# Second mixer of a two-block transformer kernel: the second value tile projected last and turned inside the attention

## What is computed

```
q, k, v, qi, ki, wi = split(h @ w_in)      # 16 query heads, 4 key heads, 4 value heads of 64; 8 index heads
q, k = rope(rmsnorm(q)), rope(rmsnorm(k));  qi = rope(qi);  ki = rope(layernorm(ki))
score[t, s] = sum_h relu(qi[t, h] . ki[s]) * wi[t, h]      # causal
sel = top_k(score[t], 128)                                  # keys kept for token t
p = softmax(q . k / 8 over the selected keys);  o = p @ v;  out = o @ w_out
```

## Time and profile before

| what | value |
|---|---|
| median of 3 runs | 2035.12 us (2034.83 to 2035.23) |
| the profiled execution's own time | 2035.02 us |
| its span in the profile | 2033.2 us |
| TensorE busy | 2019.3 us, 99% of the span |
| VectorE busy | 1569.3 us, 77% |
| ScalarE busy | 1012.6 us, 50% |
| GpSimd busy | 264.9 us, 13% |
| chain that ended last | 89% TensorE, 7% VectorE, 2% ScalarE |
| projection of the second mixer ends, its attention ends | at about 1023 and 1113 us |

### The profile page before, as it was taken

The page is one execution under the profiler, slowest core; times in us unless marked ns, Lnnn a source line. Parts: engine busy times, 40 slices in busy tenths (PEclk is TensorE's granted clock), DMA queues, the critical chain, the costliest instruction groups (busy, mean ns, idle before and its releaser), DMA issues.

```text
span 2033.2 us, 35256 instructions
## 1 busy us (share of the span) xinstructions
PE 2019.3 (99%) x12600; PEld 1763.5 (87%) x12600; DVE 1569.3 (77%) x2377; ACT 1012.6 (50%) x1798; POOL 264.9 (13%) x254
## 2 busy tenths in 40 slices
PE   9999999999999999999999999999999999999999
PEld 8999988886889998877766889998888888999987
DVE  8789876897688988775987688888777668888822
ACT  6455632568455556234577455555233234555621
POOL 0021022650200301124311200001200000000000
PEclk9999999999999999999999999999999999999999
DMA  4233476330323335734310323335836522333332
GB/s 170 91 111 104 144 257 239 122 98 2 93 78 108 109 99 176 258 115 120 100 36 1 94 83 104 103 98 179 287 129 193 171 92 78 99 103 103 106 97 87
DMA packets 76474, 245.81 MB, mean 121 GB/s; under 512 B 9408, under 2 KB 9664, under 8 KB 76256
## 3 DMA queue, kind: packets, MB, share of 16 engines
q1 hardware_dynamic: 61376, 189.60, 30.1%
q0 software_dynamic: 15008, 55.06, 8.2%
HBM read 237.74 MB, written 2.62 MB: 118 GB/s over the span
## 4 chain that ended last, share of the span: by engine, by line
PE 89%; DVE 7%; ACT 2%; issue 1%; DMA 0%; ACTq 0%; SPq 0%; DVEq 0%
PE ps L879 17%; PE ps L881 16%; PE ps L880 16%; PE ps L979 12%; PE ps L978 12%; PE ps L977 12%; DVE ps L2527 1%; PE ps L1205 1%; DVE tmp L2029 1%; DVE small L2421 1%; PE ps L1226 1%; PE ps L1243 1%; PE ps L1368 0%; DVE ssum L1997 0%; DVE score L2634 0%
## 5 line engine op out<-in xcount | busy, mean ns | idle before, releaser
L1452 ACT ACTIVATE w_hi<-w_raw 128x1024 fp32r<-128x1024 f32 (+2 forms) x231 | 211.4, 917 | 245.5 <-PE ps L881 244.9
L879 PE MATMUL ps<-h_hi,w_hi 128*128 128x512 f32 x768 | 304.4, 396 | 0.0
L881 PE MATMUL ps<-h_hi,w_lo 128*128 128x512 f32 x768 | 299.4, 390 | 0.0
L880 PE MATMUL ps<-h_lo,w_hi 128*128 128x512 f32 x768 | 299.2, 390 | 0.0
L1987 DVE TENSOR_TENSOR w_lo<-w_raw,w_hi 128x768 fp32r<-128x768 f32 (+2 forms) x196 | 196.4, 1002 | 89.5 <-ACT w_hi L1452 83.7
L979 PE MATMUL ps<-h_hi,w_lo 128*128 128x256 f32 x840 | 237.7, 283 | 0.0
L978 PE MATMUL ps<-h_lo,w_hi 128*128 128x256 f32 x840 | 237.7, 283 | 0.0
L977 PE MATMUL ps<-h_hi,w_hi 128*128 128x256 f32 x840 | 237.7, 283 | 0.0
L978 PE MATMUL ps<-t_lo,w_hi 128*128 128x256 f32 x832 | 235.5, 283 | 0.0
L977 PE MATMUL ps<-t_hi,w_hi 128*128 128x256 f32 x832 | 235.5, 283 | 0.0
L979 PE MATMUL ps<-t_hi,w_lo 128*128 128x256 f32 x832 | 235.5, 283 | 0.0
(11 more groups left out here) (393 smaller groups left out, 4538.2 us busy)
## 6 DMA issues: line engine op xcount, KB each, us to landing
w_raw<-in_gate SPq DMA_DIRECT2D x88, 512.0 KB, 3.5
w_raw<-in_up SPq DMA_DIRECT2D x88, 512.0 KB, 4.4
h_over<-in_ada_w POOLq DMA_DIRECT2D x53, 512.0 KB, 5.3
w_raw<-in_down SPq DMA_DIRECT2D x64, 384.0 KB, 3.7
ada_raw<-in_ada_w POOLq DMA_DIRECT2D x43, 512.0 KB, 4.9
w_raw<-in_down SPq DMA_DIRECT2D x64, 320.0 KB, 4.2
w_raw<-in_w_mix_c SPq DMA_DIRECT2D x24, 512.0 KB, 3.9
w_raw<-in_w_mix_b SPq DMA_DIRECT2D x17, 512.0 KB, 3.6
```

The costliest lines, as they stand in the source:

```text
L879: pe.matmul(dest, s_hi, m_hi, start=first and n == 0, stop=False)
L880: pe.matmul(dest, s_hi, m_lo, start=False, stop=False)
L881: mm = pe.matmul(dest, s_lo, m_hi, start=False, stop=last and n == len(pairs) - 1)
L1452: act.activation(w_hi[:, cut], w_raw[:, cut], ACT.Copy).then_inc(w_hi_done, 1)
```

## The change

Three things change, and nothing of what is computed.

1. vB1 becomes the last tile, so the list is ki, wi, qi0 to qi3, vB0, kB0, kB1, qB0 to qB7, vB1. The key and query tiles are projected one place earlier. vB1's product goes to bank 7, its copy to a part of `relu`, and it is turned in step 1 of the attention; the head sum of qB7 falls into vB1's job, and the roots and the table load come before ScalarE waits for that job. The unread products go to bank 6, since bank 7 holds vB1.
2. The rope of a key tile comes 5 places after the tile (before 4), so it stays in steps 12 and 13; those of the query tiles move one step earlier, to steps 11 to 17. The rope of qB7 is taken apart: one of its three operations in each of the steps 1, 2 and 3 of the attention.
3. In `TOPS_AT` steps 10 and 11 have one round less each, and steps 17 and 18, which had none, have one each. The total ahead of the attention stays at 30.

The diff, cut to its core:

```diff
-        TILES_B = ["ki", "wi", "qi0", "qi1", "qi2", "qi3", "vB0", "vB1", "kB0", "kB1"] + [f"qB{t}" for t in range(8)]
+        TILES_B = ["ki", "wi", "qi0", "qi1", "qi2", "qi3", "vB0", "kB0", "kB1"] + [f"qB{t}" for t in range(8)] + ["vB1"]
...
-            return at + 4 if t[0] == "k" else at + 2
+            if t == "qB7":
+                return at + 3
+            return at + {"kA": 4, "kB": 5}.get(t[:2], 2)
...
-                return bank(TILES_B.index(t) % 4)
+                return bank(7 if t == "vB1" else TILES_B.index(t) % 4)
...
-        TOPS_AT = {8: (0, 1), 9: (4, 1), 10: (5, 2), 11: (4, 1), 12: (0, 2), 13: (3, 0), 14: (3, 0), 15: (2, 0), 16: (2, 0)}
+        TOPS_AT = {8: (0, 1), 9: (4, 1), 10: (5, 1), 11: (3, 1), 12: (0, 2), 13: (3, 0), 14: (3, 0), 15: (2, 0), 16: (2, 0),
+                   17: (1, 0), 18: (1, 0)}
...
             for m in range(2, len(TILES_B)):
                 tile_job(TILES_B, "mixB", m, 3, betweenB)
-            betweenB(len(TILES_B), 0)
-
...
+                if pair == PAIRS_B[2]:
+                    after(pe, v_done, "vB1")
...
             def sumsB(u):
+                if u == 1:
+                    turn_tile(TILES_B, len(TILES_B) - 1)
...
-            attention(PAIRS_B, scoreB, lambda pair: pair_turn(pair, pB, T, matsB), valuesB, sumsB, "stdB", 5)
+            attention(PAIRS_B, scoreB, lambda pair: pair_turn(pair, pB, T, matsB), valuesB, sumsB, "stdB", 5, 6)
...
                 t = TILES_B[m - 1]
+                if t == "vB1":
+                    query_std("B", 8 * len(QUERIES[1]))
+                    exp_table()
+                    after(act, i_sum, IDX[-1])
                 act.wait_ge(job_done, J + m + RING)
...
-            query_std("B", 8 * len(QUERIES[1]))
-            exp_table()
-            attention(PAIRS_B, pB, T, pTB, qscB, lambda u: None)
+            def keep_last(u):
+
+                if u == 1:
+                    keep_tile("vB1", len(TILES_B) - 1, values_place(vB, 2 * TT, 2 * TT))
+
+            attention(PAIRS_B, pB, T, pTB, qscB, keep_last)
...
+            def last_rope(u):
+
+                t, before = "qB7", ROPES.index("qB7") - 1
+                if u == 1:
+                    after(dve, h_scaled, t)
+                    after_nth(dve, h_roped, before)
+                    dve.tensor_tensor(chunk(ropB, 0), straight(t), tab_cos, ALU.mult)
+                if u == 2:
+                    dve.wait_ge(*rot_sem(t))
+                    dve.tensor_tensor(chunk(ropB, 1), turned(t), tab_sin, ALU.mult).then_inc(h_sin.at(t), 1)
+                if u == 3:
+                    after(dve, h_sin, t)
+                    dve.tensor_tensor(chunk(qB, 7), chunk(ropB, 0), chunk(ropB, 1), ALU.add).then_inc(h_roped.at(t), 1)
...
-                if u == 1:
-                    head_rope("qB7", ropB, chunk(qB, 7))
+                last_rope(u)
...
-    main = tiles(np.concatenate([ki, ki, qi, vv, k, q], axis=1))
+    main = tiles(np.concatenate([ki, ki, qi, vv[:, :P], k, q, vv[:, P:]], axis=1))
```

More of the change, by code:

```diff
@@ L529, in build @@
         p_misc = Marks(sem("p_misc"), ["mem_total", "mem_spread", "conv_total", "conv_var", "conv_spread", "shift3", "ki_total", "shift4", "shift5", "shift6"])
[L531 removed]
+        TURNED_SQUARES = [t for t in SQUARES if t[:2] == "qA" or t in ("qB3", "qB4", "qB5", "qB6")]
         sq_kept = Marks(sem("sq_kept"), TURNED_SQUARES)
@@ L1093, in tile_job @@
                     after(pe, a_misc, "stdA")
+                if t == "vB1":
+                    after(pe, i_relu, IDX[-1])
                 mem = t[:2] in ("mk", "mv")
@@ L1144, in head_sum @@
                         after(pe, h_std, "kB1")
-                    if t in ("mq0", "qB6"):
-                        after(pe, sq_kept, {"mq0": "qA3", "qB6": "qB5"}[t])
+                    if t in ("mq0", "qB7"):
+                        after(pe, sq_kept, {"mq0": "qA3", "qB7": "qB6"}[t])
                     q = QUERIES[t[1] == "B"].index(t)
@@ L1179, in head_spread, with attention @@
                 mm.then_inc(h_spread.at(t), 1)
-            def attention(pairs, score, turn, values, sums, std, beside_exp):
+            def attention(pairs, score, turn, values, sums, std, beside_exp, idle_bank):
                 for u in range(len(pairs) + 5):
@@ L1185, in attention @@
                         after(pe, u_score, pairs[1])
-                        idle(beside_exp)
+                        idle(beside_exp, idle_bank)
                     if u < len(pairs):
@@ L1345, in _ @@
             take(first_job["outA"] + 1)
-            attention(PAIRS_A, scoreA, lambda pair: pair_turn(pair, pA, M, matsA), valuesA, sumsA, "stdA", 4)
+            attention(PAIRS_A, scoreA, lambda pair: pair_turn(pair, pA, M, matsA), valuesA, sumsA, "stdA", 4, 7)
             out_chunk("outA", 6, oA_hi, oA_lo, ("a", 9))
@@ L1722, in head_gain @@
                 if t == "kB0":
-                    after(act, v_turned, "vB1")
+                    after(act, v_turned, "vB0")
                 W = M if t[:2] == "mk" else T
@@ L1740, in query_std @@
                 first, last = 2 * TT * mine[0], 2 * TT * (mine[-1] + 1)
-                after(act, sq_kept, {"A": "qA3", "B": "qB5"}[which])
+                after(act, sq_kept, {"A": "qA3", "B": "qB6"}[which])
                 act.activation(qstd[:, first:last], qstd[:, first:last], ACT.Sqrt, bias=tiny[:, 0:1], scale=1.0 / HD)
```

10 lines of the change are left out of this document (5 added, 5 removed).

## The result

| | median | lowest to highest | runs |
|---|---|---|---|
| before | 2035.11 us | 2034.78 to 2035.88 | 22 |
| after | 2037.88 us | 2036.98 to 2039.39 | 22 |

The ratio is 1.0014, with a 95% interval of 1.0009 to 1.002: the change makes the kernel slower by 2.8 us, less than the 0.2% that counts as a difference, but well outside the range of the forecast. The forecast of 2033.1 us was wrong.

What follows compares the result with a forecast made beforehand. TensorE bounds the projection, VectorE the path from last product to first selection round. Pair 2's maximum 2.0 us sooner gives 2035.02 - 2.0 = 2033.0; the median lies 0.10 above, so 2033.1 us, range 2031.6 to 2035.3.

Steps and rivals of the forecast that it cites:

- The measure: Start of the attention's first selection round: a shift of it was taken to be a shift of the end.
- TensorE's list: Last product to pair 2: TensorE alone would reach pair 2 at 1026.1 against 1028.64, 2.5 us sooner.
- From the first maximum to the first round: Start of the attention: same chain as before from pair 2 on, first maximum 1025.1, first selection round near 1032.4.
- VectorE's early end: End of VectorE's work ahead of the attention: reckoned at 1024.0 instead of about 1025.0.
- What can shrink is waiting: VectorE's early ropes: the 1.50 us wait for qB6's rotated copy goes, as that copy is issued a tile earlier.
- GpSimd's splits wait for ropes that now come earlier, so they can only come sooner: GpSimd in the projection: splits are released by earlier ropes; no time was entered for this in the sum.
- Rounds moved to steps 17 and 18 cost nothing as long as VectorE ends by 1025; they are counted in its sum: VectorE late in the projection: two selection rounds moved there, entered at no extra cost.
- rival 1: VectorE not ready earlier, or the clock falls all the same: pair 2 only 0.9 or 1.3 us sooner, 2034.1; chance 0.22.
- stays at 1.00: Sign of a right forecast: the granted clock at the start of the attention does not fall.
- Rival 3: Slower: splits of jobs 15 to 20 meet ropes, 1.13 us each; four more lose 2.5 us, 2037.6; chance 0.08.
- mostly beside selection rounds: Where GpSimd's splits were said to run in the kernel before, beginning right behind a rope.
- Rival 2: Start of attention: vB1's copies and turn and the rope's parts add a wait of 1.5 to 2 us, 2035.1; chance 0.10.

Runs made afterwards that it cites:

- f1: Changed kernel with three selection rounds done early, in steps 9 and 10, and GpSimd's splits of jobs 15 to 20 one rope later: 2033.08 us.
- e3: Changed kernel with three selection rounds taken from steps 16, 17 and 18 and done in steps 9 and 10: 2034.01 us.
- e4: Changed kernel with 17 unread products instead of 5 ahead of pair 2: 2035.72 us.
- f2: Changed kernel with GpSimd's splits of jobs 15 to 20 one rope later and 9 unread products instead of 5: 2034.14 us.
- f3: Changed kernel with the table of selection rounds of the kernel before: 2034.94 us.
- f4: Changed kernel with 17 unread products and the rope of qB7 whole in step 1 of the attention: 2036.37 us.
- e1: Changed kernel with GpSimd's splits of jobs 15 to 20 waiting for the rope of the next query tile: 2034.66 us.
- g3: Kernel before with only the change's table of selection rounds: 2038.70 us.
- e2: Kernel before with GpSimd's splits of jobs 16 to 20 waiting for one rope earlier and that of job 15 for none: 2035.29 us.
- g2: Changed kernel with 11 unread products instead of 5 ahead of pair 2: 2037.24 us.

## Why the prediction was wrong

**The measure was right.** Where the clock stays up, a shift of the first selection round is a shift of the end: f1's round is 2.44 us earlier than before (aligned), its profiled time of 2033.33 less its mark of 0.77 is 2.46 below 2035.02. For the changed kernel the shifts are +1.61 and +1.55.

**TensorE's list was right.** Last product at 1022.91 aligned (forecast 1022.92), the two pairs 0.64 each, ten unread passes 1.28 (1.3), no gap in the projection, no wait for `evac` or `v_done`. Copies of vB1 and the table load stayed off the path. TensorE alone would have reached pair 2 at 1026.1 aligned, as forecast; in f1, where VectorE is no hindrance, it does at 1026.41.

**From the first maximum to the first round was right at full clock.** Forecast 1025.1 to 1032.4, or 7.3; in e3, e4, f1, f2 and f3 it is 7.37. The three parts of the rope cost nothing and save 0.46 of it (f4).

**The failing step is VectorE's early end:** "reckon the end at 1025.0 - 1.5 + 0.5 = 1024.0", and with it the first maximum at 1025.1. It came at 1027.46 aligned, 2.4 later. Its terms:
- "What can shrink is waiting", -1.5 for the copy. That wait did go. But idle time as a whole did not fall, 6.40 us against 6.29: where 1.0 less was forecast, waits for index scores (3.40 us where 0.84 stood) took its place. They were entered with 0.5.
- "GpSimd's splits wait for ropes that now come earlier, so they can only come sooner" was true and was harm: three of the six now run into a rope. I had a price in the text (1.13) and put it into a rival at 0.08 instead of the sum. VectorE's busy time grew by 0.88. By the Trainium skill ("SBUF — State Buffer", section "SBUF: two separate sides") one of the two engines locks a port that they share while the other waits; the trace agrees with 1.67 to 1.79 us where 0.69 stands otherwise, and e1, which undoes only the gate, with 1.78 us less busy time.
- The first 384-wide index score comes 0.35 later. That it is the earlier head sums that hold it is the forecast's reason, not shown by a run.

Together 1.1 + 0.9 + 0.35 = 2.35 of the 2.36.

**"Rounds moved to steps 17 and 18 cost nothing as long as VectorE ends by 1025; they are counted in its sum"** was the deeper error. I counted work, not where it lay. Steps 9 to 12 were bound in part by the arrival of index scores, so rounds there were free in part (put back in f3, the two take 0.99 us of idle time away); behind step 16 each of 1.24 us is on the way to the first maximum. f3 and g3 give this one table 2.9 and 3.4 us, the clock that falls with it included; of VectorE's start alone it is 0.96 and 1.64.

**The clock** was in rival 1 with 1.2 us, as slower unread passes. What came is another mechanism: the passes ran at full speed and so ended sooner, TensorE then stood for 3.11 us, and the clock fell under work that is read. It costs 2.2 us of the median (e4), 1.2 in the profiled execution (8.58 us from first maximum to first round instead of 7.37). The forecast named the clock as something that "stays at 1.00" and did not ask what a late VectorE would do to it.

**The rivals.** Rival 3 (slower, 0.08) had the right place and half the mechanism. It asked for four additional meetings with a loss of 2.5 us, and four more long operations there are; that the loss came out near its number is luck. They raised VectorE's busy time by 0.88 and not by 4 x 1.13, since a split that is not beside a rope is not free either. The prediction has the old splits "mostly beside selection rounds", but one, at 990.76, lay beside index sums. VectorE's timeline of the kernel before:

```profile
990.60 2.44 DVE L2620 SCALAR_TENSOR_TENSOR score<-relu,wi,score 128x512 f32<-128x512 f32 x2
```

By e2 four more such meetings cost the kernel before nothing that its time shows, and the loss of 2.8 needed the late rounds and the clock. Rival 1 named both things that happened, a VectorE that is not ready and a clock that falls (the prediction once calls the clock part of the second rival; it stands in the first), but had no case in which VectorE is later than before. Rival 2 did not happen (f4, f1).

**In sum:** 2.4 us for VectorE (from the traces) and 2.2 for the clock (from the medians) account for 4.6 of the 4.8 between 2033.1 and 2037.88; the 0.2 left is less than the 0.3 by which the median of the kernel before differs between batches of runs.

## What to carry to other kernels

Ask of each item that moves on a queue whether the engine waits for something else where it is taken out, and whether the next stage waits for it where it is put in: with the same count of instructions, two selection rounds cost some 3 us here. When a wait is removed ahead of a thin stage, look for the wait that appears one engine on, since TensorE can pay for it twice, in time and then in clock; unread products that last until the real work comes kept the clock in all runs of e4 and f2. And gates between engines that share a resource may be held by timing alone; if one side moves a step earlier, move the gate with it.

## What was not expected of the hardware

A split on GpSimd delays small VectorE operations too: 128x64 with one tensor operand, 0.19 us otherwise, took 1.31 beside one (f1), and an addition of 128x128, 0.28 otherwise, took 1.38 (e1).

In the executions that were profiled, a wait of TensorE of 1.5 to 3.1 us in a stage of short dependent instructions was followed by the granted level of 1.2 GHz. It came when work had already resumed (1.00 still from 1030 to 1031 in the changed kernel, where the wait ended at 1029.66) and stayed for some 3 us (after and g2), 7 (g3, 1030 to 1038) or 10 (e1, 1029 to 1040, of which nine whole microseconds read 0.50). Waits of 1.34 us (f3), 1.06 (e3) and 0.77 (e2) kept 1.00. But length alone does not decide: in the kernel before the clock fell to 0.85 from 1025 to 1026 and to 0.50 behind it, after a wait of 0.69 us, while e2 and g3, with the same wait of 0.69 at the same place, still read 1.00 there. It also varies between runs of one kernel, by their recorded clocks. The Trainium skill ("TensorE: Matmul & The Clock Gate", section "What's actually happening") holds that the low level is the default and activity lifts it. The rows agree so far that the level was lost behind waits and came back during work; the same thin chain of pairs that runs at 1.00 in e3 ran at 0.50 for 9 us in e1. What sets the length of the low stretch stays open, and so does why one execution loses the clock after a wait that another passes.
